# Attention kernel on one core: a tile's turned probabilities leave PSUM in one instruction per engine instead of two

## What is computed

```python
SEQ, H_B, KV_HEADS, HEAD_DIM = 1024, 8, 2, 64
def gqa_axial_attention(q, k, v, qn_g, kn_g, tables):
    q, k = rmsnorm(q per head, qn_g), rmsnorm(k per head, kn_g)
    q, k = apply_axial_rope(q, tables), apply_axial_rope(k, tables)
    # per block of 128 queries, 8 query heads on 2 key/value heads
    sc = einsum('bqkgd,bskd->bkgqs', qblk, k) * HEAD_DIM ** -0.5
    p = softmax(sc, axis=-1)
    return einsum('bkgqs,bskd->bqkgd', p, v)
# per layer:
y = concat([gmlp(...) * silu(g_a), attention(...) * silu(g_b)])
x = x + rmsnorm(y @ w_out[l], post_g[l])
```

## Time and profile before

| what | us |
|---|---|
| median of 3 runs (2455.45 to 2460.44) | 2460.04 |
| the profiled execution's own time | 2463.1 |
| its span, first to last instruction | 2461.3 |
| PE busy | 2350.2 (95%) |
| PEld busy | 1954.7 (79%) |
| DVE busy | 1079.9 (44%) |
| ACT busy | 891.5 (36%) |
| attention of layer 0, from the first max to the last PT_lo | 288.2 to 494.7 |
| attention of layer 1, the same | 877.9 to 1083.2 |

### The profile page before, as it was taken

The page is one execution under the profiler, slowest core; times in us unless marked ns, Lnnn a source line. Parts: engine busy times, 40 slices in busy tenths (PEclk is TensorE's granted clock), DMA queues, the critical chain, the costliest instruction groups (busy, mean ns, idle before and its releaser), DMA issues. The chain is left out here.

```text
span 2461.3 us, 28874 instructions
## 1 busy us (share of the span) xinstructions
PE 2350.2 (95%) x11732; PEld 1954.7 (79%) x11732; DVE 1079.9 (44%) x1463; ACT 891.5 (36%) x1397; POOL 322.9 (13%) x288
## 2 busy tenths in 40 slices
PE   7999899999999989989999899999999999989997
PEld 7888688877888768878778667777888888868885
DVE  4322488825233278861632243224434434333334
ACT  4221478723322277751533022223222222222323
POOL 0096100003047510000403000000000000000001
PEclk9999899999999989999999899999999999999999
DMA  5111000033211000021311100132111111102111
GB/s 189 50 37 52 0 1 1 1 112 128 79 52 52 18 1 1 1 86 35 139 35 52 60 1 18 37 125 89 52 51 51 51 51 37 40 35 99 64 51 77
DMA packets 102001, 129.79 MB, mean 53 GB/s; under 512 B 11574, under 2 KB 64998, under 8 KB 101894
## 3 DMA queue, kind: packets, MB, share of 16 engines
q1 hardware_dynamic: 101894, 128.30, 15.9%
HBM read 111.51 MB, written 16.78 MB: 52 GB/s over the span
## 5 line engine op out<-in xcount | busy, mean ns | idle before, releaser
L190 PE MATMUL ps<-w_hi,hT_hi 128*128 128x512 f32 (+1 forms) x1408 | 542.8, 385 | 10.6 <-DVE hT_lo L228 10.1
L191 PE MATMUL ps<-w_lo,hT_hi 128*128 128x512 f32 (+1 forms) x1408 | 539.1, 383 | 0.0
L192 PE MATMUL ps<-w_hi,hT_lo 128*128 128x512 f32 (+1 forms) x1408 | 538.6, 383 | 0.0
L180 DVE TENSOR_TENSOR w_lo<-w_raw,w_hi 128x2048 fp32r<-128x2048 f32 (+1 forms) x88 | 179.8, 2043 | 610.7 <-ACT w_hi L164 608.2
L190 PE MATMUL ps<-hT_hi,w_hi 128*128 128x512 f32 x832 | 325.3, 391 | 5.0 <-DVE X L2058 2.7
L192 PE MATMUL ps<-hT_hi,w_lo 128*128 128x512 f32 x832 | 325.0, 391 | 0.0
L191 PE MATMUL ps<-hT_lo,w_hi 128*128 128x512 f32 x832 | 325.0, 391 | 0.0
L164 ACT ACTIVATE w_hi<-w_raw 128x2048 fp32r<-128x2048 f32 (+1 forms) x72 | 118.9, 1651 | 559.7 <-PE ps L192 559.7
L190 PEld LDWEIGHTS ps<-w_hi,hT_hi 128*128 128x128 f32 x1408 | 268.4, 191 | 64.6 <-DVE hT_lo L228 10.8
L192 PEld LDWEIGHTS ps<-w_hi,hT_lo 128*128 128x128 f32 x1408 | 268.2, 190 | 51.1
L191 PEld LDWEIGHTS ps<-w_lo,hT_hi 128*128 128x128 f32 x1408 | 268.4, 191 | 50.0
(11 more groups left out here) (196 smaller groups left out, 3183.5 us busy)
## 6 DMA issues: line engine op xcount, KB each, us to landing
w_raw<-in_w_in SPq DMA_DIRECT2D x22, 1024.0 KB, 5.1
w_raw<-in_ffn_w_up SPq DMA_DIRECT2D x44, 512.0 KB, 4.8
x_mid<-X SPq DMA_DIRECT2D x24, 512.0 KB, 2.7
w_raw<-in_gla_w_in SPq DMA_DIRECT2D x12, 1024.0 KB, 5.2
w_raw<-in_ffn_w_down SPq DMA_DIRECT2D x22, 512.0 KB, 3.7
X<-in_x SPq DMA_DIRECT2D x16, 512.0 KB, 6.0
w_raw<-in_w_out SPq DMA_DIRECT2D x8, 1024.0 KB, 5.4
X<-x_mid SPq DMA_DIRECT2D x16, 512.0 KB, 6.5
```

The costliest lines, as they stand in the source:

```text
L180: engine.tensor_tensor(self.p.w_lo[:, slot, 0:size], self.p.w_raw[:, slot, 0:size], plane(self.p.w_hi[:, slot, 0:size]), ALU.subtract).the ...
L190: nc.tensor.matmul(out, a_hi, b_hi, start=first, stop=False)
L191: nc.tensor.matmul(out, a_hi, b_lo, start=False, stop=False)
L192: return nc.tensor.matmul(out, a_lo, b_hi, start=False, stop=last)
```

## The change

One pair of waits, one instruction and one semaphore count per tile take the place of two on each engine. `bank_of(half)` becomes `p_banks()`, which names both banks in one access pattern of 8 x 128, and `pt_of` names all eight key blocks of the tile. PE waits once for the pair of banks and signals once, after the eighth transpose; ACT copies 1024 values in one instruction after that; DVE subtracts 1024 values in one instruction after ACT's; PE's next turn_p waits for the whole of it. The other counts are rewritten to the same points (values waits for `2 * g + 2` instead of `4 * g + 4`, exp waits for `n - 2` turned tiles instead of `2 * n - 4` halves). No other line changes.

```diff
--- before.py
+++ after.py
@@ -776,13 +776,13 @@
 
         return 6 + n % 2 if n < 2 * KV + 2 else 6
 
-    def bank_of(half):
-
-        return prog.ps[:, 4 + half, :].rearrange("p (k q) -> p k q", k=4)
-
-    def pt_of(PT, m, half):
-
-        return PT[:, m // 2 % 2, 4 * half:4 * half + 4, m % 2 * P:(m % 2 + 1) * P]
+    def p_banks():
+
+        return prog.ps[:, 4:6, :].rearrange("p b (k q) -> p (b k) q", k=4)
+
+    def pt_of(PT, m):
+
+        return PT[:, m // 2 % 2, :, m % 2 * P:(m % 2 + 1) * P]
 
     def out_cols(g, j):
 
@@ -828,14 +828,12 @@
 
             def turn_p(m):
                 pe.wait_ge(exp_done, m + 1)
-                for half in range(2):
-                    if m >= 1:
-                        pe.wait_ge(pt_lo, 2 * m - 1 + half)
-                    for j in range(4):
-                        k = half * 4 + j
-                        mm = nc.tensor.transpose(prog.ps[:, 4 + half, j * P:(j + 1) * P],
-                                                 PR[:, m % 3, k * P:(k + 1) * P], prog.ident[:])
-                    mm.then_inc(p_turned, 1)
+                if m >= 1:
+                    pe.wait_ge(pt_lo, m)
+                for k in range(TT):
+                    mm = nc.tensor.transpose(prog.ps[:, 4 + k // 4, k % 4 * P:(k % 4 + 1) * P],
+                                             PR[:, m % 3, k * P:(k + 1) * P], prog.ident[:])
+                mm.then_inc(p_turned, 1)
 
             def values(g):
                 head = 2 * g // TT
@@ -843,7 +841,7 @@
                     pe.wait_ge(v_lo, KV)
                 if g >= 1:
                     pe.wait_ge(ot_taken, g)
-                pe.wait_ge(pt_lo, 4 * g + 4)
+                pe.wait_ge(pt_lo, 2 * g + 2)
                 for k in range(TT):
                     v = VS[:, head // (H_B // KV), k, :]
                     nc.tensor.matmul(prog.ps[:, 7, 0:256], v, PT_hi[:, g % 2, k, :], start=(k == 0), stop=False)
@@ -906,13 +904,12 @@
                     m = n - 2
                     if m >= 4 and m % 2 == 0:
                         act.wait_ge(ot_ready, m // 2 - 1)
-                    for half in range(2):
-                        act.wait_ge(p_turned, 2 * m + half + 1)
-                        nc.scalar.activation(pt_of(PT_hi, m, half), bank_of(half), ACT.Copy).then_inc(pt_hi, 1)
+                    act.wait_ge(p_turned, m + 1)
+                    nc.scalar.activation(pt_of(PT_hi, m), p_banks(), ACT.Copy).then_inc(pt_hi, 1)
                 if n < NT:
                     act.wait_ge(max_done, n + 1)
                     if n >= 3:
-                        act.wait_ge(p_turned, 2 * n - 4)
+                        act.wait_ge(p_turned, n - 2)
                     nc.scalar.activation(PR[:, n % 3, :].rearrange("p (a b) -> p a b", a=2),
                                          prog.ps[:, 2 * (n % 2):2 * (n % 2) + 2, :], ACT.Exp,
                                          bias=nmx[:, n:n + 1],
@@ -981,10 +978,9 @@
                     m = n - 2
                     if m >= 4 and m % 2 == 0:
                         dve.wait_ge(ot_ready, m // 2 - 1)
-                    for half in range(2):
-                        dve.wait_ge(pt_hi, 2 * m + half + 1)
-                        nc.vector.tensor_tensor(pt_of(PT_lo, m, half), bank_of(half), plane(pt_of(PT_hi, m, half)),
-                                                ALU.subtract).then_inc(pt_lo, 1)
+                    dve.wait_ge(pt_hi, m + 1)
+                    nc.vector.tensor_tensor(pt_of(PT_lo, m), p_banks(), plane(pt_of(PT_hi, m)),
+                                            ALU.subtract).then_inc(pt_lo, 1)
                     nc.vector.reciprocal(inv[:, m:m + 1], sm[:, m:m + 1]).then_inc(inv_done, 1)
                 if n % 2 == 1 and n >= 5:
                     g = (n - 5) // 2
```

## The result

| | before | changed |
|---|---|---|
| median, us | 2459.87 (5 runs, 2455.45 to 2460.44) | 2534.72 (5 runs, 2533.46 to 2535.52) |
| profiled execution, us | 2463.1 | 2535.52 |
| its span, us | 2461.3 | 2533.7 |

The ratio of the changed kernel to the one before is 1.0308, with a 95% interval of 1.0293 to 1.0323: 75 us slower.

A forecast was written before the change was run, and what follows sets the result against it. The prediction took PE to bound the attention stages, with ACT and DVE nearly full; +72 in short steps, -4 in long ones and +3 at the ends gave +71 us, forecast 2531 us by the median, range 2513 to 2553.

The forecast's parts named there:

- The bound now: Attention stages: PE in front, busy 19.87 of 20 us, arriving at turn_p slightly before DVE has given back the banks.
- Durations: Fused copies on ACT and DVE: PT_hi 1.04 us, PT_lo 1.22, saving some 0.06 us per tile each, nothing on the path.
- the saved overhead decides: Rival on DVE's queue: fused PT_lo saves 0.07 us a tile, 9 us in all, giving 2451; chance 0.02.
- The round: From one turn_p to the next through transposes, PT_hi, PT_lo and hand-overs: 3.52 us in sum.
- Short steps: Odd tile's turn_p to the next, only turn_o and scores: 2.36 us grows by 1.16, 62 times, +72 us.
- Long steps: Even tile's turn_p to the next, with 16 values matmuls: stay bound by PE, lose a small wait, -4 us.
- Ends: Last two tiles of each attention stage, no scores to hide in: +0.6 and +0.8 us, twice, +3 us.
- The sum: Whole kernel: short steps +72, long steps -4, ends +3, together +71 us.
- The lower bound: Round at its shortest, 3.31 us: +59 in the short steps, less 4 plus 0, about 2513 us.
- a round of 2.9 to 3.2: Rival on the short steps: PE's queue gets ahead or hand-overs are faster, +0.7 x 62, about 2500; chance 0.06.
- the clock: Rival on PE in attention: idling drops the clock to 1.2 GHz, half of the stage so costs 125 more, 2656; chance 0.03.
- crossing two banks: Rival on the fused instructions: one pays at the border of two banks, a longer round, 2553 to 2590; chance 0.03.

The follow-up runs named there:

- spread_two: The kernel before with values matmuls issued eight per step, OT in the odd step, turn_o and G two steps later: 2447.1 us, ratio 0.9947.
- act_one: The kernel before with only ACT's half of the change, one PT_hi of 1024 columns after the eighth transpose: 2506.05 us, ratio 1.0193.
- dve_one: The kernel before with only DVE's half, one PT_lo of 1024 columns, PE waiting once for both banks: 2509.92 us, ratio 1.0207.
- half_cols: The changed kernel with PT_hi and PT_lo taking only 64 of every 128 columns, a constant standing in for the rest: 2471.11 us, ratio 1.0046.
- spread_one: The changed kernel with values matmuls issued eight per step, OT in the odd step, turn_o and G two steps later: 2515.57 us, ratio 1.0229.
- spread_two_nw: spread_two without the second semaphore wait (ot_ready) on PT_hi and PT_lo of every even tile: 2448.02 us, ratio 0.9946.

## Why the prediction was right, and where a term was off

Forecast 2531, measured 2534.7, in the range of 2513 to 2553. Point by point:

- *The bound now.* Right: PE arrived at turn_p a little before the banks. spread_two shows the same from the other side: when PE hardly ever arrives early, the kernel is 13 us faster.
- *Durations.* PT_hi 1.04 forecast, 1.026 measured; PT_lo 1.22, and 1.225. The page's groups give 139.3 us busy for all PT_hi before and 131.4 after, 164.0 and 156.8 for all PT_lo: 0.06 us a tile on each, as forecast, and nothing of it on the path. (ACT's busy time as a whole fell by more, 19.5 us. Some 8.6 of that are overlap and no saving: exp starts before the PT_hi ahead of it has ended in 124 cases where it was 38, and busy time counts the stretch once.) The rival *the saved overhead decides* reckons with 0.07 a tile; 0.06 is what was measured.
- *The round.* 3.52 forecast, 3.50 to 3.51 measured. The idle time ahead of turn_p was 1.1 us in 66 cases, where 1.3 in 62 was forecast. act_one, dve_one and half_cols show that the sum of its parts holds with any of them exchanged (2.97, 3.13 and 2.54 us against 2.97, 3.15 and 2.54).
- *Short steps.* +72 forecast, +69.6 measured. The mean before was 2.38, not 2.36.
- *Long steps.* -4 forecast, -0.5 measured. The steps with the inner wait did fall, from 3.84 to 3.75 us, about 3 us in all. Against that stand the first long step of layer 1, which grew from 2.61 to 3.57 us, and the last of each layer, from 2.92 to 3.66, which the forecast had booked under the ends, with 0.6 each.
- *Ends.* +0.6 and +0.8 per layer forecast, +0.75 and +0.8 measured. The 3.66 of the last step is the even tile's round with its second wait, which the forecast left out.
- *The sum.* Against the parts of the forecast the short steps gave 2.4 us less and the long steps and ends 2.2 more (+1.2 instead of -1). That these cancel is luck; the mechanism does not hang on it. +71 was forecast on the profiled execution, and +72.4 measured between the two profiled ones, of which 70.8 are in the steps and ends. The rest of the miss is not in the kernel: the profiled execution before lay 3.2 us above its median, the profiled one after 0.8 above, so the medians differ by 74.9. The lower bound was added up wrong by 2 us: 2460 + 59 - 4 is 2515, not 2513.
- *Rivals.* The saved overhead decided nothing; a round of 2.9 to 3.2 is what each half of the change gives by itself; the clock stayed at 1.00 with PE at 16.73 of 20 us; and half_cols puts the price of crossing two banks at 9 ns or less. The rule of the Trainium skill that names large tiles and one instruction over several banks (Advanced Engine Details and Errata, The Read-Write Bubble) holds for the engine's own time (0.06 us less per tile on ACT and on DVE) and says nothing of who waits for the bank; here the latter was the whole cost. The 0.3 us per ACTIVATE that the prediction takes from the Trainium skill (ScalarE: Activation LUTs, Rules for kernel authors) is given there for an instruction whose bias is a pointer. The copies here pass no bias, so the measured 1.09 for two says nothing against that row.

What is not settled: about 1.6 us between the two spans that lie outside the two attention stages (0.6 less ahead of the first turn_p, 0.2 more between the stages, 2.1 more behind the second). They are within what runs of one kernel differ by, and their cause is not known. Why the hand-over from ACT to DVE is 0.03 us behind one PT_hi and 0.10 behind the first of two is open too.

## What to carry to other kernels

When a buffer goes round between engines (PE fills, ACT copies, DVE subtracts, PE fills again), add up the round from start to start before fusing anything on it: durations plus the hand-overs, here 0.03 to 0.15 us each. Compare it with the *shortest* step that the bounding engine has between two uses, not with its mean; here the mean step of 3.2 us hid that half of them had only 2.25 to 2.48 us of work. Pieces that are handed over one by one are a pipeline, and one large instruction undoes it; evening out the bounding engine's steps brought 13 us here without any fusing. Even then fusing was a loss of 61 us, because the round of 3.53 is longer than the evened step of about 3.05: fuse only where the round, with the large instructions in it, stays below the shortest step.

## What the runs showed of the hardware that was not expected

- A second semaphore wait on PT_hi or PT_lo delayed its start, although the second semaphore had been reached 2.7 us before: 3.65 against 3.53 us a step in spread_one, and 3.53 for all steps once the waits were gone. Over all tiles of spread_one (medians) PT_hi starts 0.10 us after the transposes' end with the second wait and 0.04 without, PT_lo 0.10 and 0.03 after PT_hi's end. On DVE this holds only behind a single PT_hi: in spread_two, with two per tile, PT_lo starts 0.10 us after the first one's end, and in spread_two_nw, without the second wait, 0.11. The wait costs only where the instruction is on the round that decides (8 us over both layers in spread_one, nothing in spread_two).
